# Output-weight products of both layers as two matrix instructions of 256 columns in place of one of 512

## The reference

```
for l in range(2):
    p = rmsnorm(x) @ w_in[l]          # mixer a | b | c | cross q | gate, 3584 columns
    l == 0: banded softmax attention over own chunk + 8 past chunks of 64, 12 heads
    l == 1: HGRN2 gated linear recurrence, 6 heads of 128
    y = concat(mixer, cross_attention(256 memory tokens)) * silu(gate)
    x = x + y @ w_out[l]              # 1024 x 1024: the product that is changed
y = rmsnorm(x, final_g)
```

## Time and profile before

| | |
|---|---|
| median of three timed runs | 2384.84 us (2383.88 to 2388.75) |
| span of the profiled execution, first to last instruction | 2376.1 us |
| outside the span, median less span | 8.7 us |
| PE busy | 2312.2 us (97%), 23787 instructions |
| PEld busy | 2094.7 us (88%), 23787 instructions |
| DVE busy | 1819.5 us (77%) |
| ACT busy | 1413.5 us (59%) |
| POOL busy | 381.0 us (16%) |

### The profile page before, as it was taken

The page is one execution under the profiler, slowest core; times in us unless marked ns, Lnnn a source line. Parts: engine busy times, 40 slices in busy tenths (PEclk is TensorE's granted clock), DMA queues, the critical chain, the costliest instruction groups (busy, mean ns, idle before and its releaser), DMA issues. The chain is left out here.

```text
span 2376.1 us, 61711 instructions
## 1 busy us (share of the span) xinstructions
PE 2312.2 (97%) x23787; PEld 2094.7 (88%) x23787; DVE 1819.5 (77%) x3555; ACT 1413.5 (59%) x3281; POOL 381.0 (16%) x585
## 2 busy tenths in 40 slices
PE   7999999999989999999999999999999989999998
PEld 4999999999967888888887999999999978888886
DVE  7889788887666656666666998797888777888885
ACT  4564666755565555555554564776757566666664
POOL 2332000000022221211112332000000112112111
PEclk9999999999999999999999999999999999999999
DMA  6886887769894222222226897886879793444442
GB/s 227 298 299 219 301 281 231 247 220 332 232 307 121 83 66 89 90 69 83 73 81 232 272 303 242 256 275 214 266 248 312 230 269 117 129 131 122 137 135 70
DMA packets 396664, 469.64 MB, mean 198 GB/s; under 512 B 39860, under 2 KB 248556, under 8 KB 396376
## 3 DMA queue, kind: packets, MB, share of 16 engines
q1 hardware_dynamic: 379832, 406.02, 54.4%
q0 software_dynamic: 14704, 54.92, 6.6%
q10 hardware_dynamic: 1840, 4.75, 0.7%
HBM read 318.77 MB, written 151.56 MB: 198 GB/s over the span
## 5 line engine op out<-in xcount | busy, mean ns | idle before, releaser
L1468 PE MATMUL pj_acc<-x_lo,pj_wh 128*128 128x256 f32 (+1 forms) x3080 | 780.9, 284 | 0.0
L1468 PE MATMUL pj_acc<-x_hi,pj_wh 128*128 128x256 f32 (+1 forms) x3080 | 780.8, 284 | 0.0
L1468 PEld LDWEIGHTS pj_acc<-x_hi,pj_wh 128*128 128x128 f32 x3080 | 578.4, 188 | 0.0
L1468 PEld LDWEIGHTS pj_acc<-x_lo,pj_wh 128*128 128x128 f32 x3080 | 578.4, 188 | 0.0
L509 ACT ACTIVATE pj_wh<-pj_wt 128x512 fp32r<-128x512 f32 x676 | 420.3, 634 | 255.9 <-DMA pj_wt<-tsum 175.1
L516 DVE SCALAR_TENSOR_TENSOR pj_wl<-pj_wt,pj_wh 128x512 fp32r<-128x512 f32 x676 | 467.0, 708 | 87.0 <-ACT pj_wh L509 79.3
L1464 PE MATMUL pj_acc<-x_hi,pj_wl 128*128 128x256 f32 (+1 forms) x3080 | 509.4, 287 | 13.8 <-DVE pj_wl L516 11.9
L1464 PEld LDWEIGHTS pj_acc<-x_hi,pj_wl 128*128 128x128 f32 x3080 | 425.3, 188 | 22.1 <-DVE pj_wl L516 19.5
L1307 DVE TENSOR_TENSOR pj_out<-pj_out,pj_acc 128x512 f32<-128x512 f32 (+1 forms) x448 | 320.8, 716 | 103.3 <-PE pj_acc L1468 69.7
L2541 DVE COPY pb_pt<-pb_SCTP 128x256 f32<-128x256 f32 (+2 forms) x266 | 115.8, 435 | 147.5 <-PE pb_SCTP L2352 74.3
L2676 ACT ACTIVATE pb_se<-pb_se,pb_mn 128x640 f32<-128x640 f32 (+4 forms) x208 | 154.6, 745 | 114.6 <-DVE pb_mn L2524 114.3
(11 more groups left out here) (371 smaller groups left out, 3992.1 us busy)
## 6 DMA issues: line engine op xcount, KB each, us to landing
pj_wt<-tsum SPq DMA_DIRECT2D x546, 256.0 KB, 3.8
proj<-pj_out SPq DMA_DIRECT2D x112, 512.0 KB, 4.2
tsum<-pj_wt SPq DMA_DIRECT2D x140, 256.0 KB, 3.2
pj_wraw<-in_w_in_dram POOLq DMA_DIRECT2D x24, 1024.0 KB, 6.6
tsum<-pj_wraw SPq DMA_DIRECT2D x56, 256.0 KB, 4.2
hg_x<-x_mid SPq DMA_DIRECT2D x17, 512.0 KB, 3.7
pb_gate<-proj SPq DMA_DIRECT2D x16, 512.0 KB, 5.1
pb_x<-in_x_prompt_dram SPq DMA_DIRECT2D x16, 512.0 KB, 3.8
```

The lines of the kernel that those rows point to most:

```text
L1468: ins = nc.tensor.matmul(BANK[j][:, 0:n], w.hi[j][:, k], x.of(y, p, j)[:, k], start=False, stop=(k == 3 and i == 1))
```

## The change

Each product of a 128 x 128 block of y with a 128 x 512 piece of the output weights becomes two, one for columns 0 to 255 of the sum and one for 256 to 511. The first product of each sum (row group 0, high times high), which also opens the sum, stays whole. The signal to VectorE is given by the last of the two last instructions.

```diff
-                        cs = slice(half * 512, half * 512 + 512)
-                        ins = nc.tensor.matmul(sum_of(job, half), (yl if part == 2 else yh)[job % 2][:, k],
-                                               (wol if part == 1 else woh)[:, group_of(job, k), cs],
-                                               start=(k == 0 and part == 0), stop=(k == KD - 1 and part == 2))
+                        for at, to in ((0, 512),) if k == 0 and part == 0 else ((0, HALF), (HALF, 512)):
+                            cs = slice(half * 512 + at, half * 512 + to)
+                            ins = nc.tensor.matmul(sum_of(job, half)[:, at:to], (yl if part == 2 else yh)[job % 2][:, k],
+                                                   (wol if part == 1 else woh)[:, group_of(job, k), cs],
+                                                   start=(k == 0 and part == 0), stop=(k == KD - 1 and part == 2 and to == 512))
...
-                        cs = slice(half * 512, half * 512 + 512)
                         g = GROUPS[s]
-                        nc.tensor.matmul(to[:], yh[:, s], woh[:, g, cs], start=(s == 0), stop=False)
-                        nc.tensor.matmul(to[:], yh[:, s], wol[:, g, cs], start=False, stop=False)
+                        whole = ((slice(0, 512), slice(half * 512, half * 512 + 512)),)
+                        halves = [(slice(at, at + HALF), slice(half * 512 + at, half * 512 + at + HALF)) for at in (0, HALF)]
+                        for ts, cs in halves if s else whole:
+                            nc.tensor.matmul(to[:, ts], yh[:, s], woh[:, g, cs], start=(s == 0), stop=False)
+                        for ts, cs in halves:
+                            nc.tensor.matmul(to[:, ts], yh[:, s], wol[:, g, cs], start=False, stop=False)
                         if s % 4 == 0:
                             pe.wait_ge(s_yl, 2 * job + s // 4 + 1)
-                        ins = nc.tensor.matmul(to[:], yl[:, s], woh[:, g, cs], start=False, stop=(s == KD - 1))
+                        for ts, cs in halves:
+                            ins = nc.tensor.matmul(to[:, ts], yl[:, s], woh[:, g, cs], start=False, stop=(s == KD - 1 and ts.stop == 512))
```

## The result

| | before | changed |
|---|---|---|
| median | 2386.24 us (6 runs, 2381.09 to 2392.03) | 2398.84 us (6 runs, 2395.38 to 2406.01) |
| ratio, as measured (the quotient of the two medians is 1.0053) | | 1.0061 [1.0047, 1.0076] |
| profiled execution: time, span | span 2376.1 us | 2398.39 us, 2396.7 us |

The change makes the kernel slower by 0.6%, where 0.27% faster was forecast; the time lies outside the forecast's range of 2374.5 to 2387.

The account below looks back on a forecast made before the run. PE was taken to bound the kernel. Span 2376.1 less 8.1 for the pairs, plus 1.1 for fetches and 0.5 for lost cover, gave 2369.6; with 8.7 around it 2378.3 us, range 2374.5 to 2387 (8 in 10).

Parts of the forecast that it names:

- The price of the pair: Output products, both layers: two 256-column pieces take 226.6 ns against 233.2 whole; 1180 pairs save 6.5 ns each, 7.7 us.
- The Trainium skill's rule: Matrix instructions on PE: N/2.4 + 2.5 ns each, so a pair costs 2.5 ns more, 3.9 us for 1564 pairs.
- Rival 1: Output products: weight loads, delayed by DVE or ACT reads, make a pair 233 ns; no gain, 2383 to 2387 us; chance 0.22.
- Exits and entries: Where output products meet other PE work: 0.9 us saved into transposes, 0.5 lost at exposed exits, 0 at entry.
- the exits into transposes: 288 places where output products give way to transposes, both stages: 3 ns saved each, 0.9 us.
- the exposed exits: 96 places where a 64-row block's load after output products is not hidden: 5 ns more each at worst, 0.5 us lost.
- Fetches: PE's instruction queue: 12 more fetches at 0.09 us each, 1.1 us lost; ends of the range 0 and 15.6 us.
- the new ones fall into the products: Low end of the fetch term, 0: added fetches land in output products, which use up 256 instructions in 14.5 us.
- the rival that had it (0.05): Added fetches and moved boundaries hit the dense products; gain gone from 0.5 us per added fetch; 2384 to 2389; chance 0.05.
- The 8.7 us around the span: Time outside the profiled span, added to the forecast span of 2369.6 us to give 2378.3.
- Cover: DVE and ACT work behind PE's products: ample room, but first tiles of each stage wait; 0.5 us lost.
- What bounds the kernel: PE, busy 97% of the span and never waiting long, so a nanosecond saved per matrix instruction comes off the span.

Follow-up runs that it names:

- e4: Changed kernel, but in the recurrence stage both pieces of a pair read the same 256 columns of the output weights; 2392.47 us (one run).
- e6: Kernel before, with pairs for the first 52 band-stage products and 28 per recurrence tile, fixing block boundaries at instructions 71, 327, 583, 839; 2415.72 us, ratio 1.013.

## Why the prediction was wrong, step by step

**The price of the pair: wrong, with its sign.** The step was "A pair costs 226.6 ns, 6.6 less than the whole", and 1180 of them were to save 7.7 us. A pair costs 236 to 237. The step took the price from 18 instructions of one stretch and held the likeness to be close. The projection has two prices and the stretch showed the lower one; the output products run at the other. By the higher, to be had from the same trace, the forecast would have had 2 x 118 less 233.2, 2.8 ns a pair, and 1564 x 2.8 = 4.4 us lost; measured are 3.8 and 3.4 ns, 5.6 us (2.9 and 2.7). The premise beside it, that the excess over streaming grows faster than the columns (19.9, 14, 6.6), falls with it: 118 is 11 above 106.7.

The Trainium skill's rule ("TensorE: Matmul & The Clock Gate", Back-to-back issue gap), which the prediction set aside, had 2.5 ns more for a pair and 3.9 us in all. Its difference was nearer than mine, though by the rule a piece would take 109 ns and a whole 216, and the trace has 118 and 233. The page calls it the gap of an isolated matmul, which the prediction did not say, and gives about 131 ns at 512 columns for a stream in which each matmul brings its weight load; that is further from the 233 here.

**Rival 1 (weight load sets the pace)** named 233 ns for a pair and 116 to 118 for a piece. Its number came true, with a margin to the worse. Its mechanism did not: it had DVE's and ACT's reads delay the load, and the pieces run at 118 with ACT idle and a single instruction on DVE (above). That the load paces them is not shown either.

**Exits and entries: small, but the exits into transposes had the wrong sign.** The 0.9 saved there hung on the price of 113.3 and fell with it. In the band stage a group of three pairs between transposes takes 12 ns longer in the middle of 224, 4 a pair, exit and entry included; at the exposed exits the 0.5 lost wasn't seen, 0.33 us before and after, to the 10 ns of the rows.

**Fetches: count right, cost wrong.** 12 more were forecast and came. They were priced at 0.09 us each, a mean over the stage, 1.1 us in all. They cost 11.2 us of waits, 0.93 per added fetch, and 3.4 of half clock behind the two longest. What failed is the sentence "the new ones fall into the products", with "luck of some 2 us either way" for the boundaries that move. The prediction divided by 59 fetches, but the waits had not been spread evenly over them: they belong to two zones of a tile, and 968 and 1060 instructions lead the boundaries through them differently. Nor did the products shelter them: the longest waits are in the products, since a boundary just behind a burst still pays for the burst. Of the range given for this term, 0 to 15.6 us, the result is at the upper end, and it is a draw: e4, with the same boundaries, had no half clock behind its two longest waits; the rival that had it (0.05) was priced up to 2389 and even so too low. e6 shows what the same step can cost, 32.8 us.

**The 8.7 us around the span: wrong.** The changed kernel's profiled execution takes 2398.39 us with a span of 2396.7, 1.7 around it. So before's profiled execution took about 2377.8, 7 us under its median: it was a lucky draw, and I took luck for a constant. All of before's other executions on record have 1.7 to 1.8 around the span as well. It did little harm here, because the sum was made as a difference to that median, but waits read in a lucky execution may be too few.

**Cover: right.** Waits for DVE and ACT didn't grow, and their busy time is the same within 0.3%. (the earlier trace rows show waits for ACT and POOL past the first tiles, not for ACT and DVE in them, as the prediction read.)

**What bounds the kernel: right.** PE does, and the added ns and the waits went into the time. That is why so small a term decided it.

## What to carry to other kernels

A price for an instruction is the distribution of its starts over the whole trace, not one clean stretch: count the levels before taking a difference of 3% from one. Where an engine issues hundreds of tiny instructions, adding instructions anywhere, even a stage earlier, moves the boundaries of its fetches; take the number of instructions per tile modulo 256 and see which bursts the boundaries meet. And a change that is to gain 0.3% can lose twice that through this alone, so a comparison of two kernels at that level should ask for it first.

## What the runs showed of the hardware that I had not expected

- PE's matrix instructions of 256 columns run at 113.3 or at 118 ns, start to start, level by level in unbroken stretches. The division changes from execution to execution; in twelve traces 48 to 1390 of the 3511 steps of layer 1's projection were at the high level.
- A fetch of 256 instructions costs PE nothing or up to 2.6 us, by its place. 102 instructions more or less in another stage made 33 us in a kernel of 2400. The fetches that PE waited for had begun 2.2 to 2.9 us before it went on.
- After standstills of 2.07 and 2.60 us the granted clock fell to 1.2 GHz for 3.4 us, starting 0.4 and 0.6 us after PE had gone on; after others, of 2.08 and 2.55 us in e4, it didn't.
- An increment of a semaphore on PE's queue, with nobody waiting for it, cost 8.6 ns at the most, by an estimate that holds some waits besides.
